# Turning normalised rows by products with a diagonal, and where the second pass and a weight split then stand

## The reference

```python
def layer_norm(x, g, b):
    xf = x.astype(F32)
    mu = jnp.mean(xf, -1, keepdims=True)
    var = jnp.mean(jnp.square(xf - mu), -1, keepdims=True)
    return ((xf - mu) * lax.rsqrt(var + LN_EPS) * g.astype(F32) + b.astype(F32)).astype(x.dtype)

def swiglu(x, w13, w2):
    g, u = jnp.split(x @ w13, 2, axis=-1)
    return (jax.nn.silu(g) * u) @ w2

# first block, layer i
h = layer_norm(DEEPNORM_ALPHA * h + mix, ln1_g[i], ln1_b[i])
h = layer_norm(DEEPNORM_ALPHA * h + swiglu(h, f_w13[i], f_w2[i]), ln2_g[i], ln2_b[i])
```

## Time and profile before

| | us |
|---|---|
| median of 3 runs (lowest, highest) | 1747.71 (1744.97, 1751.12) |
| the profiled execution's own time | 1749.66 |
| its span | 1747.9 |
| TensorE busy | 1680.7 |
| VectorE busy | 948.0 |
| ScalarE busy | 764.5 |
| GpSimd busy | 165.4 |

### The profile page before, as it was taken

One profiled execution on the slowest core, in us unless ns is written; L12 is line 12 of the kernel. 1 busy time (PEld: TensorE's weight loads), 2 busy tenths in 40 slices (PEclk: granted clock), 3 DMA queues, 4 the chain that ended last, 5 costly groups with the idle time before them and its releaser, 6 DMA issues.

```text
span 1747.9 us, 27671 instructions
## 1 busy us (share of the span) xinstructions
PE 1680.7 (96%) x11886; PEld 1539.4 (88%) x11886; DVE 948.0 (54%) x1085; ACT 764.5 (44%) x979; POOL 165.4 (9%) x170
## 2 busy tenths in 40 slices
PE   7999999999899899999999999999999999989998
PEld 6996787999777689988999899989889999879997
DVE  4664236554535565556655565556766364665543
ACT  4454333444325534433444354444655354444432
POOL 0113420000000100001000130012100020020000
PEclk8999999999999999999999999999999999999999
DMA  7553238665556786655765566645445242676652
GB/s 230 146 180 133 98 121 252 183 191 186 202 175 235 243 248 188 189 193 169 196 179 184 180 191 174 188 169 183 154 141 154 69 138 92 199 224 180 177 187 95
DMA packets 329168, 306.54 MB, mean 175 GB/s; under 512 B 11953, under 2 KB 286934, under 8 KB 328918
## 3 DMA queue, kind: packets, MB, share of 16 engines
q1 hardware_dynamic: 324246, 296.19, 55.3%
q10 hardware_dynamic: 4528, 7.54, 1.3%
q0 software_dynamic: 272, 1.05, 0.2%
HBM read 303.69 MB, written 1.05 MB: 174 GB/s over the span
## 4 chain that ended last, share of the span: by engine, by line
PE 87%; DVE 6%; ACT 3%; DMA 2%; issue 1%; POOL 1%; SPq 0%; DVEq 0%; POOLq 0%; ACTq 0%
PE ps L412 49%; PE ps L436 17%; PE ps L455 8%; ACT whi L383 2%; PE ps L473 1%; DVE wlo L389 1%; PE ps L1178 1%; PE ps L1194 1%; PE ps L1798 1%; PE ps L594 1%; DMA raw<-in_b_w_qkv 1%; PE ps L2396 1%; PE ps L2295 1%; DVE x L708 1%; DVE small L663 0%
## 5 line engine op out<-in xcount | busy, mean ns | idle before, releaser
L389 DVE TENSOR_TENSOR wlo<-raw,whi 128x2048 fp32r<-128x2048 f32 x247 | 567.7, 2300 | 408.6 <-ACT whi L383 408.5
L412 PE MATMUL ps<-ah,whi 128*128 128x256 f32 x2368 | 678.1, 286 | 7.1 <-DVE wlo L389 7.1
L412 PE MATMUL ps<-ah,wlo 128*128 128x256 f32 x2368 | 672.8, 284 | 0.0
L412 PE MATMUL ps<-al,whi 128*128 128x256 f32 x2368 | 672.8, 284 | 0.0
L383 ACT CAST whi<-raw 128x2048 fp32r<-128x2048 f32 x247 | 470.0, 1905 | 246.6 <-PE ps L436 157.1
L412 PEld LDWEIGHTS ps<-ah,whi 128*128 128x128 f32 x2368 | 457.5, 193 | 10.1 <-issue 7.1
L412 PEld LDWEIGHTS ps<-al,whi 128*128 128x128 f32 x2368 | 457.4, 193 | 1.8 <-issue 1.4
L412 PEld LDWEIGHTS ps<-ah,wlo 128*128 128x128 f32 x2368 | 457.2, 193 | 0.0
L764 ACT ACTIVATE f_sig<-ps 128x256 f32<-128x256 f32 x110 | 42.1, 383 | 359.2 <-PE ps L412 345.3
L436 PE MATMUL ps<-whi,fh 128*128 128x512 f32 x440 | 171.6, 390 | 0.0
L436 PE MATMUL ps<-wlo,fh 128*128 128x512 f32 x440 | 171.3, 389 | 0.0
(11 more groups left out here) (360 smaller groups left out, 1642.2 us busy)
## 6 DMA issues: line engine op xcount, KB each, us to landing
raw<-in_f_w SPq DMA_DIRECT2D x132, 512.0 KB, 4.6
raw<-in_w_a SPq DMA_DIRECT2D x132, 512.0 KB, 4.6
raw<-in_w_ada SPq DMA_DIRECT2D x72, 512.0 KB, 4.6
raw<-in_w_in SPq DMA_DIRECT2D x68, 512.0 KB, 4.6
raw<-in_w_b SPq DMA_DIRECT2D x66, 512.0 KB, 4.7
raw<-in_a_w_in SPq DMA_DIRECT2D x32, 512.0 KB, 5.2
raw<-in_b_w_qkv SPq DMA_DIRECT2D x24, 512.0 KB, 5.8
raw<-in_a_w_out SPq DMA_DIRECT2D x8, 512.0 KB, 4.0
```

The source lines that it names most:

```text
L389: dve.tensor_tensor(wlo[:, c % RING, :], raw[:, r % RING, :], whi[:, c % RING, :].bitcast(F32), ALU.subtract).then_inc(S("lo_ready"), 1)
L412: last = pe.matmul(out_ap, a, b, start=(i == 0), stop=(i == n - 1))
```

## The change

Turns 1 to 3 no longer transpose finished rows. TensorE first puts the offsets b into the bank (identity times the offset columns, spread over 128 tokens, 512 columns), and then adds products of `xn` with a diagonal matrix of the rows' rstd, which turns and scales at once. ScalarE makes the diagonal (`ln_diag`). The second pass still has to be done for x0, but now stands behind the turn on VectorE. For the fourth LayerNorm both passes go into the first four cuts of up2. One split of weights moves too: that of up0's cut 1, of m_qkv's cut 1 and of up1's cut 1 from before the last sums to behind the second pass, and that of up4's cut 1 from before the gate products to behind turn 8.

```diff
+    ln_diag = at("ln_diag", 74, [P, TT, P])
+    def turn_ln_pe(pe, n):
+        i = n - 1
+        for tt in range(TT):
+            pe.wait_ge(*S("ln_aggr", 2 * i + tt + 1))
+            for kh in range(2):
+                offset = col(("ln1_b", "ln2_b")[i % 2], 8 * (i // 2) + 4 * kh, 4)
+                pe.matmul(bank(4 + 2 * tt + kh, 4), ident, offset.unsqueeze(2).to_broadcast([P, 4, P]),
+                          start=True, stop=False)
+            pe.wait_ge(*S("ln_diag", 2 * i + tt + 1))
+            for kh in range(2):
+                pe.wait_ge(*S("ln_scaled", 4 * i + 2 * tt + kh + 1))
+                for k in range(4):
+                    f = (4 * kh + k) * P
+                    last = pe.matmul(ps[4 + 2 * tt + kh][:, k * P:k * P + P], xn[:, tt, f:f + P], ln_diag[:, tt, :],
+                                     start=False, stop=(k == 3))
+                last.then_inc(S("turned"), 1)
+
+    def ln_diag_act(act, n):
+        for tt in range(TT):
+            act.wait_ge(*S("ln_rstd", 2 * (n - 1) + tt + 1))
+            act.activation(ln_diag[:, tt, :], ident, ACT.Copy, scale=rstd[:, tt:tt + 1]).then_inc(S("ln_diag"), 1)
...
@@ ln_sums_of_out
         cut_ahead(dve, q.cut[1])
-        cut_ahead(dve, q.cut[2])
@@ ln_rows
-    def ln_rows(dve, n):
+    def ln_rows(dve, n, parts=range(4)):
...
+        for part in parts:
+            tt = part // 2
...
+            if part % 2 == 0:
+                dve.wait_ge(*S("ln_aggr", 2 * n + tt + 1))
+                for h in range(2):
+                    dve.scalar_tensor_tensor(xn[:, tt, half[h]], x0[:, tt, half[h]], mv[:, tt, 0:1], gb[:, 0, half[h]],
+                                             ALU.subtract, ALU.mult).then_inc(S("ln_scaled"), 1)
+            else:
+                dve.wait_ge(*S("ln_rstd", 2 * n + tt + 1))
+                for h in range(2):
+                    dve.wait_ge(*S("ln_scaled", 4 * n + 2 * tt + h + 1))
+                    dve.scalar_tensor_tensor(x0[:, tt, half[h]], xn[:, tt, half[h]], rstd[:, tt:tt + 1],
+                                             gb[:, 1, half[h]], ALU.mult, ALU.add).then_inc(S("ln_done"), 1)
@@ ffn_dve, down
-            if n or j < KF // 2 - 1:
+            if n or j < KF // 2 - 2:
                 cut_ahead(dve, c)
@@ merge_dve
-        for j in range(3):
+        for j in range(2):
             cut_ahead(dve, segs["w_out"].cut[j])
@@ block.tensor (and the same for 2 and 3)
-        turn_pe(pe, 1, x0)
+        turn_ln_pe(pe, 1)
@@ block.scalar (and the same for 2 and 3)
+        ln_diag_act(act, 1)
         turn_act(act, 1, "g_out")
@@ block.vector
         ln_sums_of_out(dve, 0, segs["g_out"])
-        ln_rows(dve, 0)
+        ln_rows(dve, 0, (0, 2))
         turn_dve(dve, 1)
+        ln_rows(dve, 0, (1, 3))
+        cut_ahead(dve, segs["g_out"].cut[2])
         cut_ahead(dve, segs["g_out"].cut[3])
...
-        ln_rows(dve, 1)
+        ln_rows(dve, 1, (0, 2))
         turn_dve(dve, 2)
+        ln_rows(dve, 1, (1, 3))
+        cut_ahead(dve, segs["down0"].cut[KF // 2 - 2])
         ada_sum_dve(dve, 3)
         cut_ahead(dve, segs["down0"].cut[KF // 2 - 1])
...
-        ln_rows(dve, 3)
         def second_rows_dve(e, j):
-            if j != UP_AT:
-                return
-            rms_dve(e, 1, x0)
+            if j < 4:
+                ln_rows(e, 3, [j])
+            if j == UP_AT:
+                rms_dve(e, 1, x0)
...
         turn_dve(dve, 8, mod_scale(4))
+        cut_ahead(dve, segs["w_out"].cut[2])
         cut_ahead(dve, segs["w_out"].cut[3])
```

More of the change, by code:

```diff
@@ L48 @@
 TAKES_OVER = {
+    "ln_diag": ("exp_s", 1),
     "gate_diag": ("diag_a", 4), "gate_row": ("diag_b", 4),
@@ L582, in turn_pe @@
             tt, kh = b // 2, b % 2
-            if n in (1, 2, 3):
-                pe.wait_ge(*S("ln_done", 4 * (n - 1) + b + 1))
-            elif n:
+            if n:
                 pe.wait_ge(*S("rows_ready", 2 * (n - 4) + tt + 1))
@@ L694, in ln_sums_of_out @@
         ln_aggr(dve, n, 4, 1)
-    def ln_rows(dve, n):
+    def ln_rows(dve, n, parts=range(4)):
         half = [slice(512 * h, 512 * h + 512) for h in range(2)]
[L699 to L709, removed]
+        for part in parts:
+            tt = part // 2
+            if part == 0:
+                dve.wait_ge(*S("gb_in", 32 * n + 32))
+            if part % 2 == 0:
[9 more added lines that the diff above has]
+                                             gb[:, 1, half[h]], ALU.mult, ALU.add).then_inc(S("ln_done"), 1)
     def ln_pool(pool, n):
@@ L2639, in _ @@
         ada_chunk_pe(pe, 15)
-        turn_pe(pe, 2, x0)
+        turn_ln_pe(pe, 2)
         ada_cols_pe(pe, 3)
@@ L2647, in _ @@
         ada_chunk_pe(pe, 29)
-        turn_pe(pe, 3, x0)
+        turn_ln_pe(pe, 3)
         ada_chunk_pe(pe, 30)
@@ L2724, in _ @@
         ada_row_act(act, 3)
+        ln_diag_act(act, 2)
         turn_act(act, 2, "up0")
@@ L2729, in _ @@
         skip_cuts(act, "m_out", range(3))
+        ln_diag_act(act, 3)
         turn_act(act, 3, "m_out")
@@ L2850, in _ @@
         ln_sums_of_out(dve, 2, segs["m_out"])
-        ln_rows(dve, 2)
+        ln_rows(dve, 2, (0, 2))
         turn_dve(dve, 3)
+        ln_rows(dve, 2, (1, 3))
+        cut_ahead(dve, segs["m_out"].cut[2])
         cut_ahead(dve, segs["m_out"].cut[3])
```

## The result

| | before | changed kernel |
|---|---|---|
| median us (lowest, highest) | 1749.41 (1744.97, 1754.78) | 1786.53 (1783.81, 1790.55) |
| span of the profiled execution | 1747.9 | 1787.0 |
| TensorE busy | 1680.7 | 1698.2 |

What follows compares the result with a forecast made beforehand. TensorE, 96% busy, bounds the kernel, so only its idle or slow-clock time counts. Terms 12.3 + 12.3 + 11.2 - 3.7 - 2.2 = +29.9 us on the profiled 1749.66 give 1779.6; the median, 1.95 lower, 1778; range 1766 to 1790.

Steps and rivals of the forecast that it cites:

- The queue: First and third turn: loads of chunks 14 and 30 wait for the late split, so TensorE stalls; +12.3 us each.
- Rival 1: Faster: the chunk's load does not hang on the late split, so the kernel takes about 1740.5 us; 3%.
- rival 4: No change: the three stalls come out at a third, say because TensorE makes them good in later waits; 2%.
- VectorE's chain: First turn: after the last low part, four second passes (2.65 us, to 288.4), then the split (2.29, to 290.7).
- The landing: Chunk 14's arrival after its issue: median 4.3 us plus an estimated 0.5, so at 295.5.
- Second turn: Down0 to m_qkv: sums follow the quarters, so m_qkv starts earlier; -3.7 us, up to 0 if cut 3 is late.
- Just in time: Second turn: m_qkv's cut 3 lands at 495.5, is split by 499.7 and needed at 500.0.
- w_out: W_out to up4: chunk 34's load waits for the late split, chunk 35 follows; up4 starts late, +11.2 us.
- The turn by products: First turn: four offset products at 0.86 us and sixteen diagonal ones at 0.22, 7.0 us at full clock.
- rivals 2 and 3: Turn products at 1.2 GHz on first and third turn, 1791 us, 7%; cheaper products, VectorE ending the turn, 1771 us, 8%.
- Down1 to up2: Fourth LayerNorm's rows move into up2's first four cuts, so TensorE's 2.20 us wait for a split goes; -2.2 us.
- The clock rule: Transposes don't count as activity for the clock, so the turn by products keeps 2.4 GHz and 7.0 us.

Runs made afterwards that it cites:

- e1: Changed kernel with the cut-1 splits of up0, up1 and up4 back where they stood before: 1744.05 us, ratio 0.9952.
- e2: Kernel before with only the cut-1 splits of up0, up1 and up4 moved behind turns 1, 3 and 8: 1783.44 us, ratio 1.0184.
- e12: e1 with only the split of up0's cut 1 behind the second pass again: 1760.76 us, ratio 1.0038.
- e7: Changed kernel with ScalarE's loads of the next gains and offsets behind its next cast at turns 1 and 3: 1780.18 us, ratio 1.0173.
- e4: Changed kernel with the late split ahead of the second pass at the three LayerNorm turns: 1770.19 us, ratio 1.0109.
- e5: e1 with the split of m_qkv's cut 1 ahead of the second pass: 1740.03 us, ratio 0.9943.
- e6: e1 with each of a turn's four offset products issued twice: 1754.80 us, ratio 1.0025.
- e9: Kernel before with only both passes of the fourth LayerNorm moved into up2's first four cuts: 1748.63 us, ratio 0.9983.
- e11: e1 with 64 transposes of the identity ahead of the first and third turn: 1755.16 us, ratio 1.0014.
- e10: e8 with the second pass back in front of the three turns and the products waiting for finished rows: 1754.75 us, ratio 1.0021.
- e3: Changed kernel, but TensorE takes chunks 14 and 30 behind cut 0 of up0 and up1, 34 and 35 behind up4's cuts 0 and 1: 1769.86 us, ratio 1.0102.
- e8: e1 with the split of m_qkv's cut 1 also back in front of the sums: 1739.58 us, ratio 0.9937.

## Why the prediction came out right, and where it was off

**The queue.** Its centre was that the split, not the products, sets the time: chunk 14 is issued behind VectorE's row work. It was issued with the split's end, e1 takes the loss away, e2 has it without the products, e12 prices one place at 15 us. Rival 1 (the load does not hang on the split) fell at the point it named, and rival 4 (the stalls are made good later) fell with e12. VectorE's chain was right to 0.1 us: forecast split end 290.7, measured 289.67 + 1.16 = 290.8 (all stages ahead ran 1.16 us earlier in this profile).

**The landing was mis-sized.** I took 4.8 us from the split's end to the chunk; it was 6.7 at the first turn. e7 shows 1.5 of these 1.9 us to be the loads of the next gains and offsets, 1 MB. They wait for the second pass, so ScalarE issues them at 287.51 and 287.88, some 2 us before the split ends, and they are still under way when the chunk is issued. My 0.5 for them was too little. What is left, 0.4 us, is not explained. That is nearly all of the +2.0 and +2.1 by which these two turns exceed the forecast.

**Second turn: the term that failed.** "Just in time" for m_qkv's cut 3 was wrong. Cut 1 and the start came as forecast (14.83 us and 8.55 behind chunk 15). Cut 3's load was issued at 501.86 and cast at 511.68, 9.8 us later; in that time chunk 16, cuts 3 and 4 and the gains and offsets were under way, 4 MB in all, issued within 6 us. TensorE waited 2.76 us, about what the term was off. The forecast had allowed for this ("up to 0 if cut 3 is late by that"). e4, which frees chunk 16's slot earlier, has neither this wait nor the loss, and e5 has its wait gone too. So the step that failed is the landing of cut 3: forecast 7.6 us behind the end of cut 1's split (487.9 to 495.5), it came 10.7 us behind it (501.0 to 511.68).

**w_out.** The start of up4 came 10.7 us late relative to chunk 32, against 11.2; the low clock behind the start, 1.9 us more, I had not counted there, though I had at the first turn. The share for chunk 35 (3.2 us) was near: it starts 2.62 us after chunk 34.

**The turn by products** took 7.3 us at full clock (forecast 7.0), which settles rivals 2 and 3 for this kernel; e6 confirms the price and that TensorE ends the turn. In e1 the first turn's stage is 0.8 us shorter than before and the third's 1.1: the products cost 7 us, and win that back from the second pass, the idle gap and the low clock, which TensorE no longer has ahead of up0.

**Down1 to up2**: -2.4 against -2.2 in the trace, and 3.0 (interval 0.7 to 5.2) by the runs of e9.

**The clock rule.** The Trainium skill ("TensorE: Matmul & The Clock Gate", Part 4: PE-mode transpose) says that the full clock doesn't engage for transposes, which don't count as the engine being busy in the same way. The trace of e11 does not agree with the first half of that where the clock is already full: 64 transposes behind full-clock work ran at it for 7.2 us. e10 shows that an idle stretch can lower the clock with products behind it. So it was most likely the idle stretch, not the transposes, that began the low stretch before; the two together were not taken apart. TensorE at the first turn before:

```profile
279.65 1.82 PE L594 MATMUL ps<-table,x 128*128 128x128 f32 x8 [2.21 <-DVE x L708]
282.30 1.97 PE L594 MATMUL ps<-table,x 128*128 128x128 f32 x8 [0.83 <-DVE x L708]
```

As to the clock's return, the traces fit the rule without proving it. At the three turns of the kernel before and of e9, TensorE resumed with transposes and had the full clock 6.9 to 8.3 us later (here from 279.65 to 286.7). Where it resumed with products or with a chunk, around the first three turns of the other kernels, it took 2.9 to 6.1 us (in e10 from 280.04 to 283.0). But each turn of transposes is broken by a second idle stretch, of 0.7 to 1.3 us, and counted from its end the return took 4.3 to 5.6 us, which lies among the times with products. My forecast had counted its 4.4 us from 282.30 in this way, without saying that TensorE had resumed at 279.65; it came near all the same (4.5 us at the first turn, 6.0 at the third).

Another 2.4 us of the miss are the clock in the token mixing (below), which the forecast does not treat; the 1.2 us ahead of the first turn go the other way, and the change does not touch that stage. So the parts of the miss, 9 us between the spans, nearly all point upwards. The measured median, 1786.5, lies in the range because its upper part had allowed for the second turn and the landings, not because the centre, 1778, was close.

## What to carry to other kernels

With a ring of raw slots and one ordered queue of loads, a split is also the release of a slot: before moving it behind other work, look up which load waits for that slot, what is queued behind this load, and which engine takes it next. Moving the taker by one step mends it in part (e3, 17 of 42 us), and so does releasing the slot ahead of only some of the work (e4, 16 us); releasing it before the turn mends it whole (e1). Other loads that are released just before share the transfer and stretch the landing (e7, 1.5 us). Work that turns and scales in one product cost TensorE more than transposes here (7.3 us at the full clock; 16 transposes at the pace of e11, 0.11 us each, would take 1.8, an estimate), and paid only where it let TensorE start earlier.

## What the runs showed that I had not expected

The granted clock falls to 0.50 even where TensorE is busy without a gap. In the changed kernel, windows 1402 to 1412 us, in the token mixing:

```profile
1402.00:1404.00 2.00, 2.00 (x17) 1.75 (x17) 0.75 (x2) 1.58 (x6) 0.00 (x0) 0.86 0.33 56
1404.00:1406.00 2.00, 2.00 (x7) 1.50 (x7) 0.96 (x3) 1.74 (x7) 0.00 (x0) 0.50 1.07 370
...
1410.00:1412.00 2.00, 2.00 (x10) 1.69 (x10) 0.42 (x1) 0.51 (x2) 0.00 (x0) 0.93 0.00 0
```

All profiles have such stretches between 1248 and 1410 us: one in before, e1, e3, e8, e11 and e12, two or three in the others, whatever was changed. TensorE is busy throughout in nearly all; those that begin at 1248.5 to 1276.8 us, in e2, e5, e9 and e10, stand behind an idle stretch of 1.9 us. What brings them about was not tried. They last 3.4 or 6.8 us at half the clock, as do others near 155 and 200 us that some profiles have and others (e1, e4, e8, e11) lack, so each moves a span by 1.7 to 3.4 us. Profiles of two kernels are therefore to be compared stage by stage, and a total only by the medians.

An idle stretch of nearly the same length lowered the clock at one turn of e10 (2.88 us) and not at another (2.79 us).
